# Expert weights through eight rooms of two transfers, and the expert steps of TensorE written out

## What is computed

```python
def expert_rows(args):
    xb, e = args
    h = jax.nn.silu(xb @ w_gate[e]) * (xb @ w_up[e])
    return h @ w_down[e]
...
shared = (jax.nn.silu(xt @ ws_gate) * (xt @ ws_up)) @ ws_down
return (routed + shared).reshape(B, T, Dm)
...
x = _layer_norm(ALPHA * x + ffn, ln2_g[l], ln2_b[l])
```

## Time and profile before

| what | value |
|---|---|
| median of 3 runs | 1268.32 us (1265.76 to 1269.01) |
| the profiled execution | 1264.77 us, its span 1263.0 us |
| mean granted TensorE clock | 0.997 of full |
| PE busy | 1222.9 us, 97% of the span, 10440 matmuls |
| DVE, ACT, POOL busy | 43%, 27%, 11% |
| expert weights | 378 + 6 loads of 1024 KB, 20.4 us from issue to landing (median; the six: 10.3) |
| chain that ended last | PE 75%, DMA 12%, DVE 4%, ACT 4%, SP's queue 2% |
| span of the expert stage | some 168.6 to 624 us and 793.7 to 1250 us |

### The profile page before, as it was taken

The page is one execution under the profiler, slowest core; times in us unless marked ns, Lnnn a source line. Parts: engine busy times, 40 slices in busy tenths (PEclk is TensorE's granted clock), DMA queues, the critical chain, the costliest instruction groups (busy, mean ns, idle before and its releaser), DMA issues.

```text
span 1263.0 us, 26524 instructions
## 1 busy us (share of the span) xinstructions
PE 1222.9 (97%) x10440; PEld 631.9 (50%) x10442; DVE 549.0 (43%) x1537; ACT 339.6 (27%) x700; POOL 134.7 (11%) x181
## 2 busy tenths in 40 slices
PE   9998999999999999999899989999999999999995
PEld 7886844334344344333389858434334444333331
DVE  4787553323323233332357866433333333232234
ACT  4667311111111111111256572111111111111111
POOL 2662210000000000000035433000000000000000
PEclk9999999999999999999999999999999999999998
DMA  9444789999999999999945529899999999999995
GB/s 350 161 184 196 291 313 388 422 422 422 422 421 420 421 421 421 421 422 421 398 163 194 210 125 374 325 373 420 422 421 423 421 420 420 421 421 421 422 421 238
DMA packets 63997, 454.44 MB, mean 360 GB/s; under 512 B 7344, under 2 KB 8112, under 8 KB 9904
## 3 DMA queue, kind: packets, MB, share of 16 engines
q1 hardware_dynamic: 63632, 452.28, 87.6%
q10 hardware_dynamic: 288, 1.05, 0.2%
HBM read 452.26 MB, written 1.05 MB: 359 GB/s over the span
## 4 chain that ended last, share of the span: by engine, by line
PE 75%; DMA 12%; DVE 4%; ACT 4%; SPq 2%; issue 1%; POOL 1%; DVEq 0%; ACTq 0%; POOLq 0%
PE banks L962 28%; PE banks L982 14%; DMA expert_weights<-in_moe_w 12%; PE banks L943 6%; PE banks L993 4%; PE banks L892 2%; SPq L436 2%; PE banks L540 2%; PE banks L541 2%; PE banks L542 2%; ACT prob L1225 1%; PE banks L832 1%; PE banks L970 1%; PE banks L833 1%; PE banks L834 1%
## 5 line engine op out<-in xcount | busy, mean ns | idle before, releaser
L962 PE MATMUL banks<-expert_weights,gathered 128*64 128x512 f32 x2000 | 448.6, 596 | 11.3 <-DMA expert_weights<-in_moe_w 11.3
L962 PEld LDWEIGHTS banks<-expert_weights,gathered 128*64 128x64 f32 x2000 | 135.8, 137 | 321.0 <-issue 278.7
L982 PE MATMUL banks<-expert_weights,hT 128*32 128x512 f32 x2048 | 233.0, 595 | 2.2 <-DVE gathered L1748 1.1
L1762 DVE TENSOR_TENSOR sig<-sig,banks 128x256 f32<-128x256 f32 x64 | 27.0, 421 | 351.7 <-ACT sig L1321 351.4
L1334 ACT ACTIVATE y_hi<-banks,gate_slot 128x512 fp32r<-128x512 f32 x126 | 86.6, 687 | 294.9 <-PE banks L982 294.9
L1772 DVE SCALAR_TENSOR_TENSOR y_lo<-banks,gate_slot,y_hi 128x512 fp32r<-128x512 f32 x126 | 94.6, 751 | 157.4 <-ACT y_hi L1334 157.4
L1321 ACT ACTIVATE sig<-banks 128x256 f32<-128x256 f32 x64 | 24.6, 384 | 424.1 <-PE banks L962 424.1
L982 PEld LDWEIGHTS banks<-expert_weights,hT 128*32 128x32 f32 x2048 | 60.2, 109 | 139.6 <-issue 136.6
L943 PEld LDWEIGHTS banks<-hot,x_part 128*128 128x128 bf16 x3072 | 93.2, 98 | 50.0 <-issue 50.0
L943 PE MATMUL banks<-hot,x_part 128*128 128x64 bf16 x3072 | 100.6, 193 | 0.0
L1387 POOL TENSOR_TENSOR piece_lo<-piece,piece_hi 128x256 fp32r<-128x256 f32 x112 | 88.0, 822 | 84.5 <-ACT piece_hi L1165 68.8
(11 more groups left out here) (219 smaller groups left out, 1254.6 us busy)
## 6 DMA issues: line engine op xcount, KB each, us to landing
expert_weights<-in_moe_w SPq DMA_DIRECT2D x378, 1024.0 KB, 20.4
piece<-in_pieces SPq DMA_DIRECT2D x32, 1024.0 KB, 5.2
quarter_ahead<-in_moe_w SPq DMA_DIRECT2D x6, 1024.0 KB, 10.3
shared_weights<-in_ws SPq DMA_DIRECT2D x2, 3072.0 KB, 12.3
ln_rows<-in_lnw SPq DMA_DIRECT2D x4, 1024.0 KB, 15.8
piece<-in_first ACTq DMA_DIRECT2D x2, 512.0 KB, 6.8
xT<-in_x_t SPq DMA_DIRECT2D x2, 512.0 KB, 6.2
x_sb<-in_x SPq DMA_DIRECT2D x1, 1024.0 KB, 15.5
```

Source lines behind the costliest of these rows:

```text
L962: mm = pe.matmul(C[e * PAIR:(e + 1) * PAIR, :], xgT[:, d, e * PAIR:(e + 1) * PAIR], w[:, e, part], start=(d == 0), stop=(d == KD - 1))
L982: mm = pe.matmul((A, B)[c][to:to + SLOTS, :], hT[:, f, of_:of_ + SLOTS], W[:, QUARTERS + c, e, f * 512:(f + 1) * 512], start=(f == 0), sto ...
```

## The change

- The places for weights are now eight rooms of two chunks each: three in `ex[0]`, three in `ex[1]`, one in the ring (where `ahead[0]` and `ahead[1]` were), and one whose first chunk is in the normalisation's rows (where `ahead[2]` was) and whose second is in `x_sb`. Sixteen chunks, where there were twelve, and fifteen at the start.
- A room's content is a third of a pair (`LOADS` is 3). Third k of a layer goes to room k mod 8 (`room_of`), all the way through the layer, so loads are issued in the order of their use. The last third goes to room 0, so that the rows of the second normalisation can be loaded to `ln_at` as before.
- Each load is still one chunk of 1 MB, with the same 8 KB per partition from the same place in HBM. Each room has two semaphores, one per chunk (`room_ld`, `rest_ld`).
- The second chunk of room 7 is loaded once `x_rest` is made and the last `add_input` has run, for which a semaphore `residual_in` is new.
- TensorE's 32 steps are all written out, and so are SP's loads. No loop is left in the stage on these two engines. The rare second pass for overfull experts is adapted to the shapes; it doesn't run with these inputs.

The diff, with the functions that it adds:

```diff
-AHEAD = 3
+LOADS = CHUNKS // 2
+ROOMS, LAST_ROOM = 8, 7
+def room_of(k):
+    return k % ROOMS if k < LOADS * PAIRS - 1 else 0
+IN_TWO = range(LOADS * PAIRS)
...
-        ahead = [place(f"quarter{q}_ahead", [P, 2, EW // CHUNKS], F32, where=moe_at) for q in range(2)]
-        ahead.append(place("quarter2_ahead", [P, 2, EW // CHUNKS], F32, where=[ln_at]))
+        ring_room = place("expert_weights_in_ring", [P, 2, 2, EW // CHUNKS], F32, where=moe_at)
+        rows_room = place("expert_weights_in_rows", [P, 2, EW // CHUNKS], F32, where=[ln_at])
+        x_room = place("expert_weights_in_x", [P, 2, EW // CHUNKS], F32, where=[ring_end])
...
+        rooms = ([ex[0][:, 2 * h:2 * h + 2] for h in range(LOADS)] + [ring_room[:, :]] + [ex[1][:, 2 * h:2 * h + 2] for h in range(LOADS)])
+        def room_chunk(k, c):
+            r = room_of(k)
+            return rooms[r][:, c] if r < LAST_ROOM else (rows_room, x_room)[c][:, :, :]
...
+        def used(k, c):
+            n, h = k // LOADS, k % LOADS
+            return (main.gu, QUARTERS * n + 2 * h + c + 1) if h < 2 else (main.dn, HALVES * n + c + 1)
...
+                    def load_half(k, c):
+                        sp.dma_start(room_chunk(k, c), of(moe_w)[0, k // LOADS, k % LOADS, c].rearrange("p (e c) -> p e c", e=2)).then_inc((room_ld, rest_ld)[c][room_of(k)], 16)
+                    def refill(k):
+                        before = max(m for m in range(k) if room_of(m) == room_of(k))
+                        for c in range(2):
+                            sp.wait_ge(*at(*used(before, c)))
+                            load_half(k, c)
...
                     for t in range(TT):
                         normalised(sp, 0, t)
-                    sp.dma_start(ahead[2][:, :, :], chunk(2, 2)).then_inc(ahead_ld[2], 16)
-                    for q in range(AHEAD):
-                        sp.wait_ge(*at(main.gu, q + 1))
-                        load_chunk(0, q, 4)
-                    refill(0, 2, range(AHEAD, CHUNKS))
-                    refill(1, 3)
-                    refill(0, 4, range(AHEAD, CHUNKS))
-                    refill(1, 5)
-                    with sp.Fori(3, PAIRS // 2) as i:
-                        for s in range(2):
-                            refill(s, 2 * i + s)
+                    load_half(7, 0)
+                    sp.wait_ge(*at(split_rest, TT))
+                    sp.wait_ge(*at(residual_in, 1))
+                    load_half(7, 1)
+                    for k in range(ROOMS, LOADS * PAIRS):
+                        refill(k)
...
-                    add_input(1, 1)
-                    for n in range(3):
-                        step(n % 2, n, n // 2, first=(n == 0), from_ahead=(n == 2))
-                    with pe.Fori(1, SHARED_FROM // 2) as i:
-                        step(1, 2 * i + 1, i)
-                        step(0, 2 * i + 2, i + 1)
-                    for n in range(SHARED_FROM, SHARED_TO):
-                        step(n % 2, n, n // 2, part=SHARED_AT.get(n), parts_read=UPS_DONE.get(n - 1, 0))
-                    with pe.Fori(SHARED_TO // 2, PAIRS // 2 - 1) as i:
-                        step(1, 2 * i + 1, i)
-                        step(0, 2 * i + 2, i + 1)
-                    step(1, PAIRS - 1, PAIRS // 2 - 1, last=True)
+                    add_input(1, 1).then_inc(residual_in, 1)
+                    for n in range(PAIRS):
+                        step(n)
```

More of the change, by code:

```diff
@@ L270, in build @@
         piece_ld = [sem(f"piece_loaded{s}", 16 * len(range(s or RING, len(STREAM), RING))) for s in range(RING)]
-        gu_ld = [[sem(f"gate_up_quarter{q}_loaded{s}", 16 * PAIRS // 2 - 16 * (q < AHEAD and s == 0)) for s in range(2)] for q in range(QUARTERS)]
-        ahead_ld = [sem(f"quarter{q}_ahead_loaded", 16) for q in range(AHEAD)]
-        dn_ld = [[sem(f"down_half{c}_loaded{s}", 16 * PAIRS // 2) for s in range(2)] for c in range(HALVES)]
+        room_ld = [sem(f"weights_loaded{r}", 16 * sum(room_of(k) == r for k in range(LOADS * PAIRS))) for r in range(ROOMS)]
+        rest_ld = [sem(f"second_half_loaded{r}", 16 * sum(room_of(k) == r for k in IN_TWO)) for r in range(ROOMS)]
+        residual_in = sem("residual_in_banks", 1)
         small_ld, ln_ld, ws_ld, wr_ld = sem("smalls_loaded", 32), sem("ln_rows_loaded", 32), sem("shared_loaded", 16), sem("router_loaded", 16)
@@ L322, in build, with landed @@
         heads_split = sem("heads_split", KD)
+        def landed(k, c):
+            before = range(k + 1)
+            if c == 0:
+                return room_ld[room_of(k)], 16 * sum(room_of(m) == room_of(k) for m in before)
+            if k in IN_TWO:
+                return rest_ld[room_of(k)], 16 * sum(room_of(m) == room_of(k) and m in IN_TWO for m in before)
+            return None
+        def used(k, c):
+            n, h = k // LOADS, k % LOADS
+            return (main.gu, QUARTERS * n + 2 * h + c + 1) if h < 2 else (main.dn, HALVES * n + c + 1)
         def piece_count(n):
@@ L463, in _ @@
                         load_piece(n)
-                    for j in range(CHUNKS):
-                        load_chunk(0, j, 0)
+                    for k in range(LOADS):
+                        for c in range(2):
+                            load_half(k, c)
                     sp.wait_ge(*at(proj, 2 * N_IN_PIECES))
-                    sp.dma_start(ahead[0][:, :, :], chunk(2, 0)).then_inc(ahead_ld[0], 16)
+                    load_half(3, 0)
                     sp.wait_ge(*at(o_sb, 8))
@@ L879, in add_input @@
                     def add_input(t, c):
-                        pe.matmul(bank[2 * t + c][:, :], alpha_i[:, :], x_sb[:, t, c * 512:(c + 1) * 512], start=True, stop=False, skip_group_check=True)
+                        return pe.matmul(bank[2 * t + c][:, :], alpha_i[:, :], x_sb[:, t, c * 512:(c + 1) * 512], start=True, stop=False, skip_group_check=True)
                     def score_tile(t):
@@ L957, in gate_up @@
                             q, part = d // each, slice(d % each * 2 * EF, (d % each + 1) * 2 * EF)
-                            if loaded is not None and d % each == 0:
+                            if d % each == 0 and loaded[q] is not None:
                                 pe.wait_ge(*at(*loaded[q]))
-                            w = early[q] if q < len(early) else W[:, q]
+                            w = W[q]
                             for e in range(2):
@@ L1004, in add_back, with step @@
                             mm.then_inc(sw.sc, 1)
-                    def step(s, n, i, first=False, last=False, part=None, parts_read=0, from_ahead=False):
+                    def step(n):
+                        s, first, last = n % 2, n == 0, n == PAIRS - 1
+                        part, parts_read = SHARED_AT.get(n), UPS_DONE.get(n - 1, 0)
                         if parts_read:
                             pe.wait_ge(*at(sh_up, parts_read))
[L1010 to L1016, removed]
+                        W = [room_chunk(LOADS * n + j // 2, j % 2) for j in range(CHUNKS)]
+                        loaded = [landed(LOADS * n + j // 2, j % 2) for j in range(CHUNKS)]
+                        gate_up(main, W, n + 1, loaded)
                         if first:
@@ L1034, in step @@
                             pe.wait_ge(*at(main.xg, 2 * (n + 2)))
-                        down(main, ex[s], n + 1, loaded=[(dn_ld[c][s], 16 * i + 16) for c in range(HALVES)])
+                        down(main, W, n + 1, loaded)
                     pe.wait_ge(*at(split_b, TT))
@@ L1066, in _ @@
                                 pe.wait_ge(*at(over_ld, 16 * k))
-                                gate_up(over, ex[0], k)
+                                W = [ex[0][:, j] for j in range(CHUNKS)]
+                                gate_up(over, W, k)
                                 turn_h(over, k)
-                                down(over, ex[0], k)
+                                down(over, W, k)
                                 add_back(over, 0, k)
```

37 lines of the change are left out of this document (13 added, 24 removed).

## The result

The changed kernel takes 1260.83 us (median of 5 runs, 1259.79 to 1261.09), the kernel before 1266.93 beside it (5 runs, 1265.76 to 1269.01). The ratio is 0.9948 with a 95% interval of 0.9933 to 0.9962: **6.1 us faster, half a percent**, where 9.8 us were forecast and a range of 1251.5 to 1265. A second set of runs on another occasion gave 0.9947 (0.9932 to 0.9962). The sign, the mechanism and the range held; the forecast gain was 1.6 times the measured one.

The account below looks back on a forecast made before the run. The load stream was taken to set each layer's end. 20.8 us won by the sixteenth room, less 5.5 us a layer for fetches, gives 9.8: 1264.77 to 1255.0, plus 3.6 for the median, 1258.5; range 1251.5 to 1265.

Parts of the forecast that it names:

- The hole and the sixteenth room: Start of the expert loop: no releases in step 2 starve the queue; one more room wins 9.8 and 11.0 us.
- rival D: First step's releases come earlier than thought, the extra room is never full: 0 to 2 us; chance 0.16 with rival B.
- my own test: After the change, no stretch under 400 GB/s between 176 and 220 us, among other signs in the profile.
- The new wait on SP: SP's queue before the room's second half: waits for the residual's last matmul, delays no refill, costs nothing.
- TensorE's side at nothing: Expert steps on TensorE: looped and unlooped both take 13.55 us, so writing them out costs or gains 0.
- The number of packets: TensorE's instruction fetches per layer: 14 become 28, and 3 of the first 54 us count too, 31.
- the price of these packets: Instruction fetches slowing the load stream: ends 2.9 and 8.2 us, the middle taken, 5.5 us a layer.
- my upper end: Fetch cost per layer, 8.2 us: 31 packets at 0.2 (6.3) plus 1.9 lost from 182 to 188 us.
- The sum: Both layers: 9.8 - 5.5 = 4.3 us and 11.0 - 5.5 = 5.5 us, together 9.8 us.
- Rival A: Fetches during the load stream are nearly free: gain 15.0 us, at most 16.3, time 1252.5; chance 0.17.
- rival B: Thin early stretches stay, only a load 1.8 us earlier per layer counts: 3.6 us, 1264.7; chance 0.16 with rival D.
- Rival C: Fetches gather on one or two DMA engines, every second adds 1.05 us: 10.2 us lost, 1278.5; chance 0.07.

Follow-up runs that it names:

- the repeat: The changed kernel unchanged, measured once more beside the kernel before: 1258.64 us, ratio 0.9947.
- before, written out: The kernel before with all 32 steps of TensorE written out and nothing else changed: 1271.61 us, ratio 1.0036.
- fourth chunk ahead: The kernel before, loops kept, with quarter 3 of pair 2 also loaded early, in the place of x_sb: 1266.42 us, ratio 0.9998.
- fifteen: The changed kernel with every load from the sixteenth on issued one release later: 1265.34 us, ratio to before 0.9988.
- one loop: The changed kernel with two buffers of one pair from pair 17 on and steps 23 to 30 a loop again: 1258.37 us, ratio to before 0.9936.
- two loops: The changed kernel with two buffers of one pair from pair 9 on, steps 9 to 12 and 23 to 30 loops: 1256.96 us, ratio to before 0.9929.

## Why the prediction came out as it did

- **The hole and the sixteenth room: right.** The queue has work from 167.8 us on, load 28 meets a queue in use, and the stretch from 204 on is full. By parts, closing the hole is worth 6.3 us and the sixteenth chunk 4.5 to 5.1. An early load alone brought nothing, and the extra room wasn't empty as rival D had it. The first stretch of my own test missed: I wanted none under 400 GB/s between 176 and 220, and from 182 to 188 it is 371.
- **The new wait on SP: right.** Load 15 lands 4.7 us after its issue, and the refills behind it go out as TensorE releases them (the first at 169.6).
- **TensorE's side at nothing: right.** 13.55 us a step in loops and out of them. The Trainium skill, "Runtime: NRT & Kernel Launch", Instruction fetch mechanics, says that crossing a 16 KiB boundary is mostly hidden and that a taken branch out of the two-page window stalls the fetch. The trace agrees as far as TensorE goes, for the first, and shows no stall of these loops. It doesn't agree for the kernel: what is hidden from TensorE comes out of the stream of the loads.
- **The number of packets: right** (31 from load 15 to load 189, 27 from 223 us on).
- **The term that was mis-sized is the price of these packets, 5.5 us a layer.** The profile shows 8.7 and 8.4, the repeat 7.3 and 7.5, 8.0 in the mean. I had the ends 2.9 and 8.2 and took the middle; it is the upper end. Load 28 shows where it goes: it lands at 197.15 + 10.42 = 207.57, and without loss would at 172.6 + 13 x 2.486 = 204.9, so 2.7 us are lost in the first 40 us of the stage, with 2 packets of q8 and 2 of q14. The other 29 of q8 cost 6.0 us, 0.21 each, just the price that I had read from the rows of before. So the part that I set too low was the shallow start: in proportion its three packets would be 0.6 us, my upper end had 1.9 more for it, and in the eight layers profiled with 16 chunks ahead it lost 1.8 to 2.9, 2.5 in the mean, with loops and without. Why it does is not shown. Not all of it can be fetches: load 16 landed 3.1 us after load 15 and load 17 2.7 after that, 0.9 us more than two loads take, and from 168 to 182 us no queue but that of the loads moved a packet:

```profile
q1 hardware_dynamic: 693, 5.14, 93.1%
```

- **The sum closes profile by profile.** With 8.7 and 8.4 us instead of twice 5.5 it is 20.8 - 17.1 = 3.7 us, and the two profiled executions are 3.7 apart. With 7.3 and 7.5 from the repeat it is 6.0, and that execution (1258.63) is 6.1 below the one of before.
- **The price of a packet is a mean of very unequal ones**, which neither my sum nor my experiments used. In layer 0 of the changed kernel four of the 161 loads after load 28 land 1.5 to 1.7 us late (29, 72, 118 and 164), 6.3 us in all; that is the whole 6.0 lost there, and the others come 2.49 us apart. Each of the four has a q8 packet in flight, the third, 11th, 19th and 27th of the 31 packets; the seven in between cost nothing. In layer 1 three of each eight share the same 1.5 us. Either way it is 0.19 a packet. Load 71 and load 72, which lands 4.2 us after it, and q8 from 316.1 to 320.1 us, between the two landings:

```profile
L463 SPq DMA_DIRECT2D expert_weights_in_ring<-in_moe_w x1: 327/327/327, 293.7 to 293.7; - x1
...
DMA to landing us min/median/max: 22.3/22.3/22.3
...
L463 SPq DMA_DIRECT2D expert_weights<-in_moe_w x1: 327/327/327, 295.4 to 295.4; - x1
...
DMA to landing us min/median/max: 24.7/24.7/24.7
...
q8 instruction: 1, 0.02, 1.7%
```

- **Rival A** (nearly free) and **rival B** (only the early load) have fallen. **Rival C** was right that a single fetch can hold up a load by a microsecond or more, and wrong about how often: it wanted every second packet, and of TensorE's it is one in eight in layer 0. GpSimd's cost 0.65 us every time. That fetches gather on one DMA engine would explain both, but it isn't shown.

| kernel | chunks ahead | packets from load 15 to 189, per layer | loss of the stream, layer 0 and 1, us | ratio to before |
|---|---|---|---|---|
| before | 15, hole, 12 | 17 | 8.0, 9.1 (hole in it) | 1 |
| before, written out | 15, hole, 12 | 31, 30 | 12.6, 12.0 (hole in it) | 1.0036 |
| fourth chunk ahead | 16, hole, 12 | 17 | 10.3, 9.9 (hole in it) | 0.9998 |
| fifteen | 15 | 31, 30 | 9.1, 6.9 | 0.9988 |
| changed kernel | 16 | 31 | 8.7, 8.4 | 0.9948 |
| changed kernel again | 16 | 31 | 7.3, 7.5 | 0.9947 |
| one loop | 16, from pair 17 on 12 | 25 | 6.6, 6.8 | 0.9936 |
| two loops | 16, from pair 9 on 12 | 23 | 6.1, 6.0 | 0.9929 |

In the five lower rows, those without a hole, the loss goes with the number of packets: 31 cost 8.0 us in the mean of the changed kernel's two profiles (fifteen has the same), 25 cost 6.7, 23 cost 6.1. That is 0.26 us for each, but 2.5 us of each sum belong to the start (with fifteen it is 4.6 and 2.5); behind load 28 a packet costs 0.16 to 0.21 us. Open remains which DMA engines a fetch queue uses and why GpSimd's packets all count: the records don't name the engine.

## What to carry to other kernels

Where one stream of loads sets the pace, look in the trace for the stretches before it is full; what counts first is that every chunk read releases the next load. One chunk more ahead brought nothing while releases were skipped, and 4.5 to 5.1 us once none was. Deep buffering is needed only until the queue has work in store: here sixteen chunks up to pair 8 and twelve with loops after it gave the lowest time of those tried. Code written out is not free in such a kernel even when no engine waits for it, because its fetches ride on the DMA engines that carry the loads.

## What was not expected of the hardware

- A packet of instructions costs a saturated stream of 1 MB loads more than its bytes. A packet of TensorE's (16 KB) cost about 0.2 us in the mean, where 16 KB at 421 GB/s are 0.04 us, and this mean is one packet in eight that costs 1.5 us (changed kernel, layer 0).
- A packet of GpSimd's (8 KB, 0.3 us by its record) cost 0.65 us every time once the queue was full. 224 KB of instructions on an otherwise idle engine, in each of two layers, made the kernel 2.1% slower.
